# Low parts of the value rows made on VectorE instead of GpSimd, and GpSimd's activation fetches grouped by quads of picks

## What is computed

```
q = (xb @ wq) ...; scores against 2 x 128 sub-keys; 16 best of 16 x 16 candidates for each of 8 heads
idx = i1 * 128 + i2                      # 128 experts per token, out of 128 x 128
gsm = softmax(best)
act = gelu(einsum('td,thkd->thk', xb, u_tab[idx]))
out = einsum('thk,thkd->td', gsm * act, v_tab[idx])
```

## Time and profile before

| | |
|---|---|
| median of 3 runs | 4794.67 us |
| the profiled execution, its own time | 4797.76 us |
| the span of its trace | 4796.0 us |
| granted TensorE clock, mean over the span | 0.969 |
| TensorE busy | 4458.9 us, 93% |
| VectorE busy | 3310.5 us, 69% |
| ScalarE busy | 1176.9 us, 25% |
| GpSimd busy | 2571.5 us, 54% |
| bytes moved, highest of the page's 40 slices of the span | 289 GB/s |
| value rows, `w_in<-in_v`, 256 loads of 512 KB | median 5.9 us from issue to landing |

### The profile page before, as it was taken

One profiled execution on the slowest core, in us unless ns is written; L12 is line 12 of the kernel. 1 busy time (PEld: TensorE's weight loads), 2 busy tenths in 40 slices (PEclk: granted clock), 3 DMA queues, 4 the chain that ended last, 5 costly groups with the idle time before them and its releaser, 6 DMA issues.

```text
span 4796.0 us, 76065 instructions
## 1 busy us (share of the span) xinstructions
PE 4458.9 (93%) x27516; PEld 4027.5 (84%) x27516; DVE 3310.5 (69%) x6141; ACT 1176.9 (25%) x1696; POOL 2571.5 (54%) x1462
## 2 busy tenths in 40 slices
PE   7888999999999999999789889999999999999996
PEld 6758999999999877777577689999999998877775
DVE  6872299779998577777734422992799984555555
ACT  2052011123233222222133420111232322222222
POOL 2413455644444688888731134555444446778874
PEclk9879999999999999999898999999999999999998
DMA  5401244557777877778510012444577778777774
GB/s 198 168 1 58 72 121 121 191 125 157 160 159 156 289 273 273 270 277 280 206 70 24 23 58 72 121 121 121 126 156 161 160 156 272 262 262 262 262 259 148
DMA packets 823653, 797.69 MB, mean 166 GB/s; under 512 B 566513, under 2 KB 601041, under 8 KB 822898
## 3 DMA queue, kind: packets, MB, share of 16 engines
q1 hardware_dynamic: 175248, 500.38, 31.2%
q10 hardware_dynamic: 603106, 159.70, 15.5%
q0 software_dynamic: 45056, 134.38, 8.7%
HBM read 640.41 MB, written 153.89 MB: 166 GB/s over the span
## 4 chain that ended last, share of the span: by engine, by line
PE 50%; POOL 18%; ACTq 8%; issue 7%; DVE 6%; DMA 6%; ACT 4%; DVEq 0%; POOLq 0%
PE acc L514 14%; PE acc L516 13%; PE acc L515 13%; POOL w_lo L487 10%; POOL found L463 5%; DMA pick_act<-act_p,where_i 5%; ACTq L1047 4%; ACTq L1080 4%; POOL pick_act L469 3%; PE aux L729 2%; ACT w_hi L1113 1%; ACT gates L1097 1%; PE aux L572 1%; DVE ag L1539 1%; PE aux L679 1%
## 5 line engine op out<-in xcount | busy, mean ns | idle before, releaser
L514 PE MATMUL acc<-a_hi,w_hi 128*128 128x320 f32 x5296 | 1670.1, 315 | 45.5 <-DVE a_lo L1287 32.5
L516 PE MATMUL acc<-a_hi,w_lo 128*128 128x320 f32 x5296 | 1641.0, 310 | 0.2 <-issue 0.2
L515 PE MATMUL acc<-a_lo,w_hi 128*128 128x320 f32 x5296 | 1640.6, 310 | 0.0
L514 PEld LDWEIGHTS acc<-a_hi,w_hi 128*128 128x128 f32 x5296 | 999.6, 189 | 50.9 <-issue 34.6
L515 PEld LDWEIGHTS acc<-a_lo,w_hi 128*128 128x128 f32 x5296 | 999.8, 189 | 1.4 <-issue 0.2
L516 PEld LDWEIGHTS acc<-a_hi,w_lo 128*128 128x128 f32 x5296 | 998.2, 188 | 0.5 <-issue 0.5
L438 POOL TENSOR_TENSOR w_lo<-w_in,w_hi 128x1024 fp32r<-128x1024 f32 (+1 forms) x345 | 902.1, 2615 | 27.6
L454 POOL CAST w_hi<-w_in 128x1024 fp32r<-128x1024 f32 x256 | 309.8, 1210 | 1044.3 <-DMA w_in<-in_u 1044.3
L487 POOL TENSOR_TENSOR w_lo<-w_in,w_hi 128x1024 fp32r<-128x1024 f32 x256 | 655.1, 2561 | 201.7 <-ACT w_hi L1113 198.4
L1525 DVE SCALAR_TENSOR_TENSOR one_b<-iota_b,picks_t 128x384 bf16<-128x384 bf16 x1024 | 629.8, 615 | 0.0
L1523 DVE TENSOR_SCALAR one_a<-iota_b,picks_t 128x128 bf16<-128x128 bf16 x1024 | 579.6, 566 | 56.6 <-PE aux L729 54.6
(11 more groups left out here) (246 smaller groups left out, 5682.7 us busy)
## 6 DMA issues: line engine op xcount, KB each, us to landing
w_in<-in_u SPq DMA_DIRECT2D x256, 512.0 KB, 4.1
w_in<-in_v SPq DMA_DIRECT2D x256, 512.0 KB, 5.9
gate_s<-gates ACTq DMA_DIRECT2D x64, 1024.0 KB, 14.1
ag<-act_s SPq DMA_DIRECT2D x256, 256.0 KB, 4.2
ag<-gate_s SPq DMA_DIRECT2D x256, 256.0 KB, 5.0
act_s<-a_out ACTq DMA_DIRECT2D x184, 256.0 KB, 3.7
act_s<-tmp ACTq DMA_DIRECT2D x72, 256.0 KB, 3.2
w_in<-in_in SPq DMA_DIRECT2D x32, 512.0 KB, 5.8
```

Source lines behind the costliest of these rows:

```text
L514: pe.matmul(out, wh, hi[:, k, n], start=(k == 0), stop=False)
L515: pe.matmul(out, wh, lo[:, k, n], start=False, stop=False)
L516: return pe.matmul(out, wl, hi[:, k, n], start=False, stop=(k == kt - 1))
```

## The change

GpSimd no longer makes the low parts of the value rows in the value stage; VectorE does, in a new `low_v` at the end of each chunk's work (chunks 0 to 2 ahead of everything, 3 to 5 beside chunks 0 to 2, and from chunk 6 on each beside itself), counted in a new semaphore `lo_v` for which TensorE waits. `lo_done` then counts the splits of GpSimd alone, so all waits on it use `split_by_pool(n)`, which leaves out the value chunks of the layer before. GpSimd only fetches: activations in groups of four picks at the head of each quad, from the third quad on after `part_ready` says that the activations of two quads before have been used; rows as before, each once pick k-8 has been added.

```diff
+        def split_by_pool(n):
+
+            return n + 1 - NKEY * CHUNKS[n][0]
...
-            def low(l, n, slot, size):
-                pool.wait_ge(hi_done, n + 1 - NKEY * l)
+            def low(count, slot, size):
+                pool.wait_ge(hi_done, count)
...
-                for c in range(NKEY):
-                    if c == 6:
-                        for s in range(4):
-                            pool.wait_ge(a_st[s], 32 * A_ALL[s] * (l + 1))
-                        for k in range(FOUND):
-                            fetch_act(l, k)
-                    slot = (VC[l] + c) % SPLIT
-                    pool.wait_ge(hi_v, NKEY * l + c + 1)
-                    pool.tensor_tensor(w_lo[:, slot, :], landing(slot), w_hi[:, slot, :].bitcast(F),
-                                       ALU.subtract).then_inc(lo_done, 1)
-                    if c >= FOUND:
-                        fetch_row(l, c)
-                        fetch_act(l, c)
+                for s in range(4):
+                    pool.wait_ge(a_st[s], 32 * A_ALL[s] * (l + 1))
+                for k in range(PICKS):
+                    if k % 4 == 0 and k >= 8:
+                        pool.wait_ge(part_ready, 2 * OCTETS * l + k // 4 - 1)
+                    if k % 4 == 0:
+                        for j in range(k, k + 4):
+                            fetch_act(l, j)
+                    if k >= FOUND:
+                        fetch_row(l, k)
...
-                pe.wait_ge(lo_done, PRODUCTS[m][4] + 1)
+                pe.wait_ge(lo_done, split_by_pool(PRODUCTS[m][4]))
...
                 def chunk_ready(i, u):
                     pe.wait_ge(p_lo, NKEY * l + u + 1 + SPLIT * i)
-                    pe.wait_ge(lo_done, VC[l] + u + 1 + SPLIT * i)
+                    pe.wait_ge(lo_v, NKEY * l + u + 1 + SPLIT * i)
...
+                def low_v(i, u):
+
+                    slot = (VC[l] + u) % SPLIT
+                    dve.wait_ge(hi_v, NKEY * l + u + 1 + SPLIT * i)
+                    dve.tensor_tensor(w_lo[:, slot, :], landing(slot), w_hi[:, slot, :].bitcast(F),
+                                      ALU.subtract).then_inc(lo_v, 1)
+
...
                         add_row(q, half, u % 4, first and u % 4 == 0)
                     low_p(i, u)
+                    if not (isinstance(i, int) and i == 0):
+                        low_v(i, u)
+                    elif u < 3:
+                        low_v(0, u + 3)
+                    elif u > 5:
+                        low_v(0, u)
...
+                for u in range(3):
+                    low_v(0, u)
                 for u in range(4):
                     chunk(0, u)
```

More of the change, by code:

```diff
@@ L231, in build @@
         v_done, v_taken, v_sum = sem("v_done"), sem("v_taken"), sem("v_sum")
-        hi_v, where_ready = sem("hi_v"), sem("where_ready")
+        hi_v, lo_v, where_ready = sem("hi_v"), sem("lo_v"), sem("where_ready")
         found_in = [sem(f"found_in{i}") for i in range(FOUND)]
@@ L444, in split_chunk @@
                 pool.tensor_copy(w_hi[:, slot, 0:size], landing(slot, size)).then_inc(hi_done, 1)
-                low(CHUNKS[n][0], n, slot, size)
+                low(split_by_pool(n), slot, size)
             def split_loop(l):
@@ L454, in split_loop @@
                         pool.tensor_copy(w_hi[:, n % SPLIT, :], landing(n % SPLIT)).then_inc(hi_done, 1)
-                        low(l, n + SPLIT * i, n % SPLIT, 1024)
+                        low(split_by_pool(n) + SPLIT * i, n % SPLIT, 1024)
             rows_of_v = a["v"].rearrange("l c p n -> (l c p) n")
@@ L707, in experts @@
                     for u in range(SPLIT):
-                        expert(UM[l] + u, (UC[l] + u) % SPLIT, UC[l] + u + 1 + SPLIT * i,
+                        expert(UM[l] + u, (UC[l] + u) % SPLIT, split_by_pool(UC[l] + u) + SPLIT * i,
                                (UM[l] + u) // 2 + (SPLIT // 2) * i)
                 for c in range(SPLIT * EARLY, SPLIT * EARLY + BRIDGE):
-                    expert(UM[l] + c, (UC[l] + c) % SPLIT, UC[l] + c + 1, (UM[l] + c) // 2)
+                    expert(UM[l] + c, (UC[l] + c) % SPLIT, split_by_pool(UC[l] + c), (UM[l] + c) // 2)
                 pe.wait_ge(picks_ready, l + 1)
@@ L742, in late @@
                             c = SPLIT * (EARLY + k) + BRIDGE + u
-                            expert(UM[l] + c, (UC[l] + c) % SPLIT, UC[l] + c + 1 + 2 * SPLIT * i,
+                            expert(UM[l] + c, (UC[l] + c) % SPLIT, split_by_pool(UC[l] + c) + 2 * SPLIT * i,
                                    (UM[l] + c) // 2 + SPLIT * i, BUILT, next_four)
```

## The result

The changed kernel takes 4618.96 us (median of 4 runs, 4617.18 to 4622.93) against 4795.49 us for the kernel before on the same chip; ratio 0.9627, 95% interval 0.9615 to 0.9639. Forecast: 4612, range 4604 to 4640. The profiled execution took 4617.94 us, with a span of 4616.1 us and a mean granted clock of 0.976.

The account below looks back on a forecast made before the run. GpSimd's queue was taken to pace the value stages; with TensorE setting the pace, 101.1 + 2.8 + 4.2 + 72.5 + 2.9 = 183.5 us leave the 4796.0 us span, giving 4612.5 and a forecast of 4612, range 4604 to 4640.

Parts of the forecast that it names:

- the circle through its late fetch: Value stages: a quad's last activation, fetched behind GpSimd's last low part, holds VectorE 4.64 us before parts, delaying GpSimd's next.
- the waits before the last four chunks: TensorE idle 22.83 and 17.95 us until all four chunks are ready, called most of the loss in one place.
- 101.1 and 72.5 us of waiting: Gains in layers 0 and 1 over the first 124 chunks, with TensorE at 5.44 us a chunk throughout.
- 2.8 and 2.9 us at the low clock: Gains in the last four chunks of layers 0 and 1, whose long matmuls follow the long idle time.
- the 4.2 us before the transposes: Layer 0, after the last four chunks: TensorE's 4.2 us wait for the added rows would go.
- The upper bound: low_v at GpSimd's 2.41 us: VectorE at 5.73 us a chunk in layer 0, costing 36 us, 4648; VectorE rival, chance 0.05.
- The start: low_v of chunks 0 to 2 ahead of form costs nothing; without cover at most 4 us a layer.
- The new wait on VectorE's queue: low_v waits for high_v, holding up the next form, add_row and low_p; hidden some five chunks ahead of TensorE.
- the 29 us to spare: Value rows to low_v take some 9.4 us after c-8 finishes; TensorE wants the chunk 38 us after it.
- Transfers: Rival: layer 0's value stage wants 315 GB/s at DMA share 0.91, so transfers bind; 4634 to 4673, chance 0.08.
- Landings: Rival: landings grow from 6.1 us to over 18, so the circle through p_lo binds; 4711 at 20 us, chance 0.03.
- VectorE and GpSimd keeping each other out: Rival: fetches can't run beside two-input VectorE instructions, so their times add in the value stages; 193 us slower, 4988, chance 0.03.

Follow-up runs that it names:

- e1: Kernel before, with activations fetched in fours two quads ahead from pick 8 on, GpSimd still making the low parts; 4669.57 us, ratio 0.9716.
- e2: Changed kernel without the grouping: GpSimd fetches the row and then the activation of each pick, one by one; 4620.81 us, ratio 0.9620.
- e8: Changed kernel run once more, nothing edited; 4618.43 us, ratio 0.9616.
- e3: Changed kernel with one more VectorE instruction, same operation and operands, before each low_v, written to an unread buffer; 4642.73 us, ratio 0.9672.
- e6: Changed kernel with low_v right behind form, ahead of add_row and low_p, from chunk 8 on; 4725.81 us (one run).
- e4: Changed kernel with 256 KB more loaded from HBM for each chunk from 8 on, into an unread buffer; 4616.71 us, ratio 0.9615.
- e5: Changed kernel with a GpSimd subtraction of 128x1024 on constants for each pick from 8 on, into an unread buffer; 4866.95 us (one run).
- e10: Changed kernel with two GpSimd memsets of 128x1024 for each pick from 8 on, into an unread buffer; 4620.51 us (one run).

## Why the prediction was right

*The bound.* GpSimd's queue and the circle through its late fetch were read rightly as what set the stages, and TensorE's 5.44 us a chunk as what would: with the circle alone broken, 131 us went (e1), and with the low parts gone from GpSimd, all of it (e2). Both stages came out at 674.7 us, where the sum had 674.7. One reading was wrong and did no harm, since the sum used the whole difference: the waits before the last four chunks were not "most of the loss", but 22.83 of 101.1 us and 17.95 of 72.5.

*The terms.* 101.1 and 72.5 us of waiting went in full, and so did 22.83 and 17.95 us in front of the last four chunks within them. The 2.8 and 2.9 us at the low clock and the 4.2 us before the transposes went too. Not in the sum: behind that wait TensorE had run at the low clock a second time (granted clock 0.62 from 2395 to 2402 us), which gave 2.4 us more. From the first transpose to the start of the last sums over squares, layer 0 took 2414.11 - 2395.38 = 18.73 us before and 2308.71 - 2292.35 = 16.36 us after.

*The 3.6 us by which the span missed* (4616.1 for 4612.5) are 5.0 us ahead of the first value stage and 1.0 between the stages (from those last sums to layer 1's first value product, 1585.8 us against 1584.8), less these 2.4. The first goes with the attention's clock; the cause of the second I did not look for. The median, 4618.96, is 7.0 us over the forecast. The other 3 us are the step from the span to the median: I went from 4614.3 down to 4612, because the profiled execution of the kernel before lay 3.1 us over its median, while that of the changed kernel lay 1.0 under its own. The gain in medians was 4795.49 - 4618.96 = 176.5 us in the result and 4800.6 - 4618.4 = 182 us for the same two kernels in e8; the forecast was 183.5, so it is high by 1 to 7 us.

*`low_v`* was taken at 1.28 us and takes 1.23. The upper bound was tried with e3: as much VectorE work as a `low_v` of 2.4 us costs 24 us, where I had put 36.

*The start* cost nothing: 1.50 us before the first value product in both layers, as before.

*The new wait on VectorE's queue* came out free, but one half of my reason was wrong. I argued from the 29 us to spare; e6 has the same loads and slots, and lost 107 us. What keeps the wait free is that `add_row` and `low_p` stand between `form` and `low_v` and cover ScalarE's two instructions, so it does not come in each chunk in full. I had that row (`high_v`, 1.04 us) only as part of a latency.

*The rivals.* Transfers (0.08): the linear scaling was good for the rate, 312 and 285 GB/s for 315 and 287 foreseen, with shares of 0.87 and 0.81 for 0.91 and 0.85; it was wrong to read the share, or one stretch at 1.00, as a ceiling (e4: 365 GB/s). The Trainium skill (SBUF — State Buffer, Summary: rules for kernel authors) gives about 358 GB/s; e4 passed it on one core. Landings (0.03): they did not grow; value rows landed in 4.4 us in layer 0, 6.1 before. VectorE and GpSimd keeping each other out (0.03): this is real, but it is about arithmetic, not fetches. By the Trainium skill (SBUF — State Buffer, Who interferes with whom) a VectorE instruction with two SBUF inputs contends with a GpSimd instruction that reads SBUF and not with one that only writes: e5 and e10 agree, at 4867 and 4621 us. (The fetch that I put inside an `add_row` began 0.23 us ahead of it; they ran together for 0.73 us.) Its part in the kernel before was larger than I gave it. I had read one `form` of 3.27 us and taken VectorE's other instructions for undisturbed, but from 1600 to 2395 us of the kernel before they are (busy us, mean ns):

```profile
L1578 DVE SCALAR_TENSOR_TENSOR total<-found,part_now,total 128x1024 f32<-128x1024 f32 x127 | 234.6, 1847 | 4.1 <-DVE part_now L1564 3.1
L1539 DVE TENSOR_TENSOR ag<-ag 128x512 f32<-128x512 f32 x127 | 164.1, 1292 | 0.0
L1553 DVE CUSTOM_DVE_ANT_0 unread_v<-w_mod_v,c_all 128x1024 f32<-128x1024 f32 x64 | 141.6, 2213 | 1.1
```

`add_row`, `form` and the modulation product took 1.85, 1.29 and 2.21 us there, against 1.31, 0.69 and 1.22 in the changed kernel. What VectorE got back was more than the price of `low_v`: in layer 0 it is busy 4.43 us a chunk with it, and was busy 602.79 us over the first 124 chunks, 4.86 a chunk, without.

## What to carry to other kernels

When two engines' queues form a circle, breaking any one link may give most of the gain (131 of 182 us by an earlier fetch alone), so measure the parts singly before crediting the larger one. For an engine that gets new work, add up its busy time and its recurring waits for one round and compare with the bound's pace; a lead hides only waits that do not recur. Arithmetic moved off GpSimd pays twice where VectorE runs instructions with two SBUF inputs beside it.

## What the hardware showed that I had not expected

A GpSimd subtraction on whose result nobody waits made the kernel 248 us slower, with VectorE full (671 of 680 us) and TensorE waiting for its `low_v`. A memset on GpSimd leaves two-input VectorE instructions alone and holds up a VectorE copy of 128x2 numbers for up to 1.73 us. The DMA share was 1.00 at 321 GB/s before the stage and 0.99 at 365 GB/s in e4, so it says that transfers were in flight, not that no more could be. And the same attention code ran at a mean granted clock of 0.63, 0.74 or 0.82 in different programs, and the first value product came up to 17 us later where it was lower.
